# Two mixture-of-experts loops: the hidden block turned once summed, and three steps moved at an expert's end

## What is computed

```python
def swiglu(h, w_gate, w_up, w_down):
    a = jnp.einsum("bsd,df->bsf", h, w_gate)
    u = jnp.einsum("bsd,df->bsf", h, w_up)
    return jnp.einsum("bsf,fd->bsd", jax.nn.silu(a) * u, w_down)

for e in range(N_EXPERTS):
    y = y + gates[..., e:e + 1] * swiglu(h, w_gate[e], w_up[e], w_down[e])
```

## Time and profile before

| what | value |
|---|---|
| median of 3 runs | 2469.22 us (2465.05 to 2471.34) |
| the profiled execution, whole | 2465.34 us |
| its span, first to last instruction | 2463.3 us |
| PE busy | 2308.1 us, 94% of the span |
| DVE busy, ACT busy | 1780.3 us (72%), 1378.1 us (56%) |
| the small stages, about | 155 to 434 us, 662 to 939 us |
| the large stage, about | 1656 to 2440 us |
| chain that ended last | PE 76%, DVE 13%, ACT 5%, issue 3% |

### The profile page before, as it was taken

One profiled execution on the slowest core, in us unless ns is written; L12 is line 12 of the kernel. 1 busy time (PEld: TensorE's weight loads), 2 busy tenths in 40 slices (PEclk: granted clock), 3 DMA queues, 4 the chain that ended last, 5 costly groups with the idle time before them and its releaser, 6 DMA issues.

```text
span 2463.3 us, 39708 instructions
## 1 busy us (share of the span) xinstructions
PE 2308.1 (94%) x14770; PEld 2068.1 (84%) x14770; DVE 1780.3 (72%) x2016; ACT 1378.1 (56%) x1522; POOL 70.2 (3%) x122
## 2 busy tenths in 40 slices
PE   7889999998899999988999998889999999999997
PEld 6789999877799998977899897778788887788876
DVE  5577775646777775885566688558888888888886
ACT  4455654445455653464433346437777777777775
POOL 0100000101000002000000200000000000000000
PEclk9999999999999999999999999989999999999999
DMA  7349999631399995634355652319899999998993
GB/s 266 127 151 364 366 374 327 171 107 51 113 359 375 376 353 127 211 101 135 120 181 170 160 183 91 132 36 361 324 331 390 337 357 374 329 390 330 338 394 116
DMA packets 253818, 609.51 MB, mean 247 GB/s; under 512 B 11217, under 2 KB 103201, under 8 KB 229009
## 3 DMA queue, kind: packets, MB, share of 16 engines
q1 hardware_dynamic: 247776, 590.84, 66.1%
q0 software_dynamic: 5248, 13.25, 2.4%
q10 hardware_dynamic: 560, 2.10, 0.2%
HBM read 605.11 MB, written 1.05 MB: 246 GB/s over the span
## 4 chain that ended last, share of the span: by engine, by line
PE 76%; DVE 13%; ACT 5%; issue 3%; DVEq 2%; DMA 1%; ACTq 0%; POOLq 0%
PE psum L137 15%; PE psum L139 15%; PE psum L138 15%; PE psum L2332 10%; PE psum L2368 9%; PE psum L2356 2%; DVE weight_ring_rounded L116 2%; DVE h_cf L3229 1%; ACT weights_high_rounded L2066 1%; PE psum L936 1%; ACT scores L970 1%; PE psum L2885 1%; PE psum L2015 1%; DVE weight_ring_rounded L2071 1%; PE psum L621 1%
## 5 line engine op out<-in xcount | busy, mean ns | idle before, releaser
L2071 DVE TENSOR_TENSOR weight_ring_rounded<-weight_ring,weights_high_rounded 128x2048 fp32r<-128x2048 f32 x264 | 603.7, 2291 | 101.5 <-ACT weights_high_rounded L2066 101.4
L2066 ACT ACTIVATE weights_high_rounded<-weight_ring 128x2048 fp32r<-128x2048 f32 x264 | 504.9, 1917 | 157.3 <-PE psum L139 142.9
L2429 DVE TENSOR_TENSOR weight_ring_rounded<-weight_ring,weights_high_rounded 128x2048 fp32r<-128x2048 f32 x128 | 293.0, 2292 | 96.8 <-ACT weights_high_rounded L2424 96.8
L137 PE MATMUL psum<-weights_high_rounded,scores_rounded 128*128 128x512 f32 (+1 forms) x768 | 291.2, 379 | 8.6 <-DVE weight_ring_rounded L2071 4.5
L139 PE MATMUL psum<-weights_high_rounded,scores_rounded 128*128 128x512 f32 (+1 forms) x768 | 287.0, 374 | 0.0
L138 PE MATMUL psum<-weight_ring_rounded,scores_rounded 128*128 128x512 f32 (+1 forms) x768 | 286.3, 373 | 0.0
L2332 PE MATMUL psum<-weights_high_rounded,scores_rounded 128*128 128x256 f32 x1024 | 262.6, 294 | 5.6 <-issue 3.3
L139 PE MATMUL psum<-weights_high_rounded,xT_rounded 128*128 128x512 f32 (+3 forms) x688 | 259.6, 377 | 0.0
L2332 PE MATMUL psum<-weight_ring_rounded,scores_rounded 128*128 128x256 f32 x1024 | 252.4, 284 | 0.0
L2368 PE MATMUL psum<-xT_high,weight_ring 128*128 128x128 f32 x2048 | 240.4, 276 | 7.3 <-DVE xT_high L2500 4.0
L2424 ACT ACTIVATE weights_high_rounded<-weight_ring 128x2048 fp32r<-128x2048 f32 x128 | 244.3, 1908 | 0.0
(11 more groups left out here) (580 smaller groups left out, 4123.5 us busy)
## 6 DMA issues: line engine op xcount, KB each, us to landing
weight_ring<-in_moe_w_gate_dram SPq DMA_DIRECT2D x152, 1024.0 KB, 6.0
weight_ring<-in_moe_w_up_dram SPq DMA_DIRECT2D x152, 1024.0 KB, 8.4
weight_ring<-in_moe_w_down_dram SPq DMA_DIRECT2D x152, 1024.0 KB, 8.3
weight_ring<-in_w_in_dram SPq DMA_DIRECT2D x20, 1024.0 KB, 7.2
weight_ring<-in_ffn_w_gate_dram SPq DMA_DIRECT2D x11, 1024.0 KB, 5.3
weight_ring<-in_ffn_w_up_dram SPq DMA_DIRECT2D x11, 1024.0 KB, 5.4
weight_ring<-in_ffn_w_down_dram SPq DMA_DIRECT2D x11, 1024.0 KB, 4.9
weight_ring<-in_w_out_dram SPq DMA_DIRECT2D x8, 1024.0 KB, 5.1
```

Source lines behind the costliest of these rows:

```text
L137: nc.tensor.matmul(out, lh, rh, start=start, stop=False)
L2066: self.c.nc.scalar.activation(ring.high(self.s0 + q, 1, SLOT), ring.view(self.p0 + q, 1, SLOT), ACT.Copy).then_inc(ring.high_ready, 1)
L2071: self.c.nc.vector.tensor_tensor(ring.low(self.p0 + q, 1, SLOT), ring.view(self.p0 + q, 1, SLOT), ring.high(self.s0 + q, 1, SLOT).bitcast( ...
L2429: self.c.nc.vector.tensor_tensor(ring.low(tile, 1, SLOT), ring.view(tile, 1, SLOT), ring.high(s, 1, SLOT).bitcast(F32), ALU.subtract).then ...
```

## The change

Small stage: ACT copies only the lower 64 rows (what the low part of the tokens gives), DVE adds the upper 64 to them (`rows_summed`), ACT takes the SiLU and DVE the product with slots still in rows, and `turn` is 2 transposes of the finished hidden block; ACT copies the turned block to `hidden`. So ACT and DVE do their elementwise work before the turn and not behind it. `twice` is gone; half of the new block's rows are zeroed once. In a step the token window goes ahead of the weight split of expert x+3, and DVE's `write(x)` moves from the start of step x+1 to the end of step x.

Large stage: the turn of step 4 comes behind all gate products of the last step; on DVE the next expert's `window_rest` comes ahead of the copy L2146. The rewritten table in `order` gives ACT and DVE the same order as before. In the first layer's mixer two pairs of semaphores become one pair, with the same waits.

```diff
@@ SplitExpert.tensor
         for j in range(steps - 1):
             if j >= 1:
                 pe.wait_ge(*self.made(c.sig("hidden_ready"), j - 1, i))
-            first(self.gate(j + 1), j + 1, 0, lambda: turn(j))
             if j < steps - 2:
+                first(self.gate(j + 1), j + 1, 0, lambda: turn(j))
                 third(j)
                 first(self.up(j + 1), j + 1, 2)
             else:
+                first(self.gate(j + 1), j + 1, 0)
+                turn(j)
                 first(self.up(j + 1), j + 1, 2)
                 third(j, lambda: turn(j + 1))
@@ SplitExpert.vector
+        if next_window:
+            next_window()
         self.used(dve, self.p0 + self.down(self.steps - 1), i)
         nc.vector.tensor_copy(self.rows[:, 512:], c.psum[:, 5, :]).then_inc(self.rows_dve.sem, 1)
         if next_window:
-            next_window()
             self.low(dve, 1, i + 1)
@@ SmallExperts.turn
-        pe.wait_ge(*self.of(self.rows_taken, x, 0))
+        pe.wait_ge(*self.of(self.rows_ready, x, 0))
...
-        for a in range(2):
-            for m in range(2):
-                at = (2 * a + m) * self.W
-                last = nc.tensor.matmul(psum[:, 2 + x % 2, at:at + self.W], blocks[:, a, m, :], self.twice, start=True, stop=True)
+        blocks = self.hidden_rows.rearrange("s (f m) -> s m f", m=2)
+        for m in range(2):
+            last = self.c.nc.tensor.transpose(self.c.psum[:, 2 + x % 2, m * P:(m + 1) * P], blocks[:, m, :], self.c.ident[:, :])
@@ SmallExperts.scalar_step
-            nc.scalar.activation(self.squashed, c.psum[:, 2 + x % 2, 0:2 * self.W].rearrange("p (m s) -> p m s", m=2),
-                                 ACT.Silu).then_inc(self.squash_done.sem, 1)
+            nc.scalar.activation(self.hidden[:, x % 2, :, 0:self.W], c.psum[:, 2 + x % 2, 0:2 * P].rearrange("p (m s) -> p m s", m=2)[:, :, 0:self.W],
+                                 ACT.Copy).then_inc(self.hidden_ready.sem, 1)
...
-            nc.scalar.activation(self.rows[:, (x + 1) % 2, :], c.psum[:, (x + 1) % 2, :], ACT.Copy).then_inc(self.rows_taken.sem, 1)
+            nc.scalar.activation(self.rows[0:self.W, (x + 1) % 2, :], c.psum[self.W:, (x + 1) % 2, :], ACT.Copy).then_inc(self.lows_taken.sem, 1)
...
+        if 0 <= x + 1 < n:
+            act.wait_ge(*self.of(self.rows_summed, x + 1, i))
+            nc.scalar.activation(self.squashed_rows, self.rows[0:self.W, (x + 1) % 2, 0:CH], ACT.Silu).then_inc(self.squash_done.sem, 1)
@@ SmallExperts.vector_step
-        if x >= 1:
-            write(x - 1)
...
+        if 0 <= x + 1 < n:
+            rows = self.rows[0:self.W, (x + 1) % 2, :]
+            dve.wait_ge(*self.of(self.lows_taken, x + 1, i))
+            nc.vector.tensor_tensor(rows, c.psum[0:self.W, (x + 1) % 2, :], rows, ALU.add).then_inc(self.rows_summed.sem, 1)
...
+        if 0 <= x + 1 < n:
+            dve.wait_ge(*self.of(self.squash_done, x + 1, i))
+            nc.vector.tensor_tensor(self.hidden_rows[0:self.W, :], self.squashed_rows, self.rows[0:self.W, (x + 1) % 2, CH:],
+                                    ALU.mult).then_inc(self.rows_ready.sem, 1)
+        if 0 < x + 3 < n:
+            self.low(dve, x + 3, 0, i)
+        if x >= 0:
+            write(x)
```

More of the change, by code:

```diff
@@ L1293, in low_stats @@
         dve.drain()
[L1294 removed]
+        nc.vector.tensor_scalar(low_var, c.stats[:, 1:3, 0:TT, 1:2], LN_EPS, None, ALU.add).then_inc(*summed.up())
     def low_root(act):
[L1297 to L1298 removed]
+        act.wait_ge(*summed.at(1))
+        nc.scalar.activation(low_rstd, low_var, ACT.Sqrt).then_inc(*rooted.up())
     def make_angles(dve):
@@ L1353, in v_root @@
     def v_root(act):
-        act.wait_ge(*v_summed.at(1))
-        nc.scalar.activation(v_rstd, v_var, ACT.Sqrt).then_inc(*v_rooted.up())
+        act.wait_ge(*summed.at(2))
+        nc.scalar.activation(v_rstd, v_var, ACT.Sqrt).then_inc(*rooted.up())
     def v_finish(dve):
-        dve.wait_ge(*v_rooted.at(1))
+        dve.wait_ge(*rooted.at(2))
         inverse_root(c, v_rstd, v_var, c.newton[:, 0:TT, :])
@@ L2078, in order @@
         ups_done = {self.up(j) + self.tiles(j) - 1: j for j in range(self.steps)}
-        turns = {self.gate(j + 1) if j + 1 < last else self.gate(j + 1) - 1: j for j in range(last)}
+        turns = {self.gate(j + 1): j for j in range(last)}
         turns[self.down(last - 1)] = last
@@ L2085, in order @@
                 squash(squashes[q])
-            if q in turns and turns[q] != last - 1:
+            if q in turns:
                 part(turns[q])
@@ L2091, in order @@
                 next_split(0)
-            if q in turns and turns[q] == last - 1:
-                part(turns[q])
             if squash_first and q in squashes:
@@ L2269, with __init__ @@
     W = 64
-    def __init__(self, c, p0, n, unroll, xg, outT, twice, tiles, landed, used, cnt, off):
-        self.c, self.p0, self.n, self.unroll, self.xg, self.outT, self.twice = c, p0, n, unroll, xg, outT, twice
+    def __init__(self, c, p0, n, unroll, xg, outT, tiles, landed, used, cnt, off):
+        self.c, self.p0, self.n, self.unroll, self.xg, self.outT = c, p0, n, unroll, xg, outT
         self.gate_tile, self.down_tile = tiles
@@ L2532, in vector @@
         self.c.nc.vector.memset(self.hidden, 0.0)
+        self.c.nc.vector.memset(self.hidden_rows, 0.0)
         dve.drain()
         self.steps(dve, self.vector_step, after_first)
-        self.vector_end(dve)
-    def vector_end(self, dve):
-        n, c = self.n, self.c
-        o = self.offset(dve, n - 1, 0)
-        made = c.psum[:, 4 + 2 * ((n - 1) % 2):6 + 2 * ((n - 1) % 2), :].rearrange("p b (k s) -> p (b k) s", k=4)
-        def small():
-            self.used(dve, self.down_tile(n - 1), 0)
-            c.nc.vector.tensor_copy(self.outT[:, :, bass.ds(o, self.W)], made[:, :, 0:self.W]).then_inc(self.written.sem, 1)
-        def wide():
-            self.used(dve, self.down_tile(n - 1), 0)
-            c.nc.vector.tensor_copy(self.outT[:, :, bass.ds(o, TOK)],
-                                    c.psum[:, 4:8, :].rearrange("p b (k s) -> p (b k) s", k=2)).then_inc(self.written.sem, 1)
-        self.by_width(dve, n - 1, 0, small, wide)
 def split_rows(c, rows, ready=None):
@@ L2607, in sparse_experts @@
     if ahead:
-        twice = sb("twice", [P, SmallExperts.W])
         picked = [x.rearrange("p t (q k) -> p t k q", k=KD) for x in rows]
@@ L2634, in _ @@
         nc.vector.tensor_tensor(member[:, :, :], oh[:, :, 0, :], oh[:, :, 1, :], ALU.add).then_inc(*joined.up())
-        if ahead:
-            nc.vector.tensor_tensor(twice[:, :], c.ident[:, 0:SmallExperts.W], c.ident[:, SmallExperts.W:], ALU.add)
         weigh(dve)
@@ L2754, in sparse_experts @@
     if ahead:
-        way = SmallExperts(c, p0, n, unroll, xg, outT, twice[:, :], (gate_tile, down_tile), landed, used, cnt_i, off_i)
+        way = SmallExperts(c, p0, n, unroll, xg, outT, (gate_tile, down_tile), landed, used, cnt_i, off_i)
     else:
```

44 lines of the change are left out of this document (18 added, 26 removed).

## The result

| what | before | after |
|---|---|---|
| median of 5 runs, us | 2469.15 (2465.05 to 2471.34) | 2450.57 (2444.47 to 2453.57) |
| ratio to before, 95% interval | | 0.9933 (0.9921 to 0.9944) |
| the profiled execution, whole, us | 2465.34 | 2447.6 |
| its span, us | 2463.3 | 2445.5 |

The change gains 18.6 us. The prediction was 50.5 us of gain, with a range of 2405 to 2440 us: the time lies above the range.

The account below looks back on a forecast made before the run. PE was taken to bound the kernel. Gains of 42 (small stages, 44.0 - 2), 6.8 and 1.7 sum to 50.5 us: profiled 2465.3 to 2414.8, plus 3.9 for the median, 2418.7 us; range 2405 to 2440.

Parts of the forecast that it names:

- The turn, 0.85 to 0.14: Small stage, PE: 2 transposes replace 8 records per expert, 0.14 us instead of 0.85, gaining 0.71 per expert.
- The chain has 1.2 us of slack: Small stage: copy, sum, SiLU and product finish 4.3 us behind the up products; PE comes after 5.49, cost nothing.
- 44.0 us for 62 turns: Small stages: the 0.71 us gained per turn, over 2 x 31 turns, gives 44.0 us.
- growing "issue" waits: Small stage, sign of being wrong: PE's issue waits grow as transfers fill the gap in which code now arrives; no size.
- The dry gap closes: Small stage DMAs: the queue's dry spell from 306.0 to 307.2 us shrinks and closes; PE asks for 413 GB/s.
- The first expert, 1.0 us a layer: Small stages, expert 0: no down products cover the chain; wait 2.3 us against 1.3 before, net loss 1.0 a layer.
- Large stage, the turn, 6.8: Large stage, turn of step 4: PE's 0.84 us wait for the hidden block goes in 8 places; gain 6.8, bounds 3.5 and 6.8.
- Large stage, the window, 1.7: Large stage, DVE's window ahead of the copy: 4.1 us in 7 places less 2.4 returning; gain 1.7, bounds 0 and 4.1.
- 1: Small stage: transfers can't go beyond the present 364 GB/s, total 2461 us, chance 0.06; half way 2426 us, chance 0.10.
- 2: Small stage turn: slow transposes, 0.43 us for the turn, total 2437 us; chance 0.08.
- 3: Small stage: the chain before the turn is late and PE waits for it, slower than before, 2485 us; chance 0.06.
- 4: Large stage: ACT's fetch waits at the change of experts vanish, 5 to 7 us better, 2412 us; chance 0.08.

Follow-up runs that it names:

- the pair without the branch: `before_nowide` and `after_nowide`: the kernels before and after, each without PE's small-stage branch for experts of over 64 tokens; 2451.01 and 2410.45 us.
- down8: Kernel after, loading one sixteenth of each small expert's down tile and using it for all down products (the rest not computed); 2424.53 us.
- before_down8: Kernel before, loading one sixteenth of each small expert's down tile and using it for all down products (the rest not computed); 2456.29 us.
- after_nowide: Kernel after, with the never-taken branch for experts of over 64 tokens left out of PE's code in both small stages; 2410.45 us.
- prime: Kernel after, with one SiLU of two columns added at the start of ACT's small stream, so table loads fall earlier; 2444.96 us, one run.
- idle: Kernel after, with ten products whose result nobody uses on PE ahead of the first turn of each small stage; 2441.83 us, one run.
- turn_only: Kernel before, with only the large stage's turn moved and the window's order as before; 2459.7 us, one run.
- best2: `best1` with PE's code in the large stage split too: one look at the largest token count, wide branches out of the narrow stream; 2410.93 us.
- best1: Kernel after, complete: PE tests the largest token count once per small stage, branched stream first, branch-free one behind; early SiLU on ACT; 2405.84 us.
- before_nowide: Kernel before, with the branch for experts of over 64 tokens left out of PE's code in both small stages; 2451.01 us.
- after_down: Kernel after, loading half of each small expert's down tile and using that half twice (the other half not computed); 2440.08 us.

## Why the prediction was wrong, step by step

- *The turn, 0.85 to 0.14*: right, 0.16; the period fell by 0.68, forecast 0.71.
- *The chain has 1.2 us of slack*: right, 4.2 us long (forecast 4.3) against 5.5; no turn but the first of a layer waits for it.
- *44.0 us for 62 turns*: this is the step that failed. It took the 0.24 us beyond 8.33 in each expert as a constant that stays when PE gets faster. It was PE waiting for code, and it grew by 11.0 and 11.4 us in the two layers. The measured gain of the 60 periods is 18.4 us (9.3 and 9.0 by the layers), where the turn gives 40.8, as the pair without the branch shows. The prediction had named growing "issue" waits as a sign of being wrong, as transfers fill the gap in which code arrives. The traffic of the weights is some 6 of the 11 us by `down8` and `before_down8`, and the cause of the rest is open. The sign had no price in the sum and no chance among the rivals, though the earlier trace rows held its first 2.5 us.
- *The dry gap closes*: some 400 GB/s were forecast and 378 measured, at a share of 0.98, since PE's stalls hold back its requests; without them, in `after_nowide`, it is 401 at 1.00. Transfers were no bound.
- *The first expert, 1.0 us a layer*: mis-sized, 3.8 and 3.4. The wait was 4.6 us, forecast 2.3; in `prime`, without the two table loads of 1.28, it is 2.0, so the chain itself was sized well and the loads were left out. Behind the wait PE's clock stood at half for some 6 us, 2.0 us by `idle`, of which the prediction did not think.
- *Large stage, the turn, 6.8*: the mechanism is right, the wait is gone; the size was too small, and above its upper bound of 6.8. The stage gained 8.8 in all and 9.7 in `turn_only` (one run). PE's waits for a split ahead of L137 also fell, from 4.5 to 3.4 us; the remaining 1 to 2 us is not traced.
- *Large stage, the window, 1.7*: nothing, the lower bound. Behind the wait for L2104 stood PE's own branch, as long as that wait, and behind the branch the split of the next tile. That 6.8 + 1.7 comes near the 8.8 of the stage is luck: the turn gave all of it.
- *Rivals*: 1 is refuted by the 401 GB/s, 2 by the 0.16, 3 by the slack; 4 did not come: ACT's issue waits between 1690 and 2440 us are 13.4 us, 13.9 before. In `best2` they are 3.3, and its stage is no faster than that of `best1`, so a gain of 5 to 7 us isn't seen there either.

The account: 50.5 forecast, less 22.4 for the stalls, less 5.2 at the first experts, less 1.7 for the window, less 1.8 for a turn of 0.68 in place of 0.71, and 2.0 more in the large stage, leaves 21.4; the medians gave 18.6 and the profiled spans 17.8. The rest of some 3 us lies in stages that the change does not touch: 2.1 us of it are there at 57 us, and `before_nowide`, with no change there at all, is late by 2.2 at the same place.

## What to carry to other kernels

An "issue" wait of the engine that bounds the stage is a term of the sum: look what the instruction queue does beside it, and don't carry it over as a constant when the engine gets faster. In this unrolled stream, code that never ran was fetched like code that ran; a rare path is better put in a stream of its own behind one test than between each two steps. And where a change lets an engine wait several microseconds at a stage's start, price the clock and the table load too.

## What the hardware showed that was not expected

- 64 more products per expert that are never executed cost 223 us, 3.5 us for each of the 64 experts, the fallen clock included. The Trainium skill (Runtime: NRT & Kernel Launch, "Instruction fetch mechanics") says that code is fetched in 16 KiB blocks in sequence, and that a taken branch out of the fetched window stalls the engine. The packets here are of that size and most stalls end at the first product behind a jump, so the trace agrees; a few sit inside a block of products. I had not weighed it.
- The stalls fell from 18.0 and 16.5 to 6.3 and 6.7 us a layer when the weights' bytes fell by 31%, but only to 16.7 and 15.2 when they fell by 17%. Of the latter two, 12.4 us lie in three long periods with a fallen clock.
- Weights came at 413 GB/s over 60 us and 401 over 231 us. The Trainium skill (DMA: Bandwidth & Descriptors, "Where 436 GB/s comes from") has about 358 as the limit from HBM; these rows disagree.
- PE's wait of 4.6 us was followed by some 6 us at a granted clock of 0.50 (1.2 GHz); with products in its place the clock stayed at 1.00.
- The clock fell behind stalls too: after the three of 2.1 to 3.0 us in `after_down` it stood at 0.50 for a time, and each such period took 3.8 to 4.5 us more than 7.65. In `after` the stalls of the periods stay under 1.9 us, and the clock between 177.06 and 419.50 us is 1.00.
- ACT's waits go with code as well, as the prediction supposed: its four issue waits of 3.0 to 3.8 us at the changes of expert end 2.2 to 2.9 us after a 16 KB packet of another instruction queue (q14) starts, in `before` and in `after`.
